# Differential attention: softmax weights combined in one pass on VectorE, weight splits held back on GpSimd, and the gate's SiLU computed through tanh

## The reference

```python
q, k, v, g_attn, x_lru, g_lru = split(rmsnorm(x) @ w_in)     # 8 heads; q, k: 2 x 64 per head; v: 128
for i in range(8):                                           # 128 queries against (i + 1) * 128 keys
    s = einsum(q_i, k[:end]) * 64 ** -0.5                    # two score maps c = 0, 1 per head
    p = softmax(where(causal, s, -inf))
    w = p[:, :, 0] - lam * p[:, :, 1]
    out_i = w @ v[:end]
o = rmsnorm(out, subln_g) * (1 - lam_init)
y_attn = o * silu(g_attn)
```

## Time and profile before

| what | value |
|---|---|
| timed runs | 3614.07, 3614.57 (median), 3616.83 us |
| profiled execution, first to last instruction (span) | 3615.4 us |
| PE busy | 3342.6 us (92%) |
| DVE busy | 1509.8 us (42%) |
| ACT busy | 867.8 us (24%) |
| POOL busy | 952.1 us (26%) |
| mean granted TensorE clock | 0.958 |

### The profile page before, as it was taken

One profiled execution on the slowest core, in us unless ns is written; L12 is line 12 of the kernel. 1 busy time (PEld: TensorE's weight loads), 2 busy tenths in 40 slices (PEclk: granted clock), 3 DMA queues, 4 the chain that ended last, 5 costly groups with the idle time before them and its releaser, 6 DMA issues.

```text
span 3615.4 us, 40852 instructions
## 1 busy us (share of the span) xinstructions
PE 3342.6 (92%) x15618; PEld 2741.2 (76%) x15618; DVE 1509.8 (42%) x1960; ACT 867.8 (24%) x1359; POOL 952.1 (26%) x514
## 2 busy tenths in 40 slices
PE   6999889887797998989999999889999989999999
PEld 5777777776585777768788888768787768888887
DVE  6775555556535566630121223222612542323232
ACT  4454334343202323221122222211201020101010
POOL 2331111111131221113222222134233323333332
PEclk9999999998998999889999999999999989999999
DMA  3220000000244111101211221231112101111112
GB/s 124 96 70 30 30 25 30 25 30 12 83 136 149 36 52 70 53 24 46 98 47 56 71 62 55 68 106 59 46 47 85 55 30 49 50 46 46 52 46 75
DMA packets 83705, 214.19 MB, mean 59 GB/s; under 512 B 7024, under 2 KB 33264, under 8 KB 83456
## 3 DMA queue, kind: packets, MB, share of 16 engines
q1 hardware_dynamic: 48176, 167.27, 14.1%
q10 hardware_dynamic: 35408, 45.24, 4.0%
HBM read 193.44 MB, written 19.04 MB: 59 GB/s over the span
## 4 chain that ended last, share of the span: by engine, by line
PE 79%; DVE 12%; ACT 4%; issue 3%; DMA 1%; ACTq 0%; PEld 0%; POOL 0%; DVEq 0%; PEldq 0%; POOLq 0%
PE proj_bank L208 20%; PE proj_bank L210 20%; PE proj_bank L209 20%; PE aux_banks L208 2%; PE aux_banks L209 2%; PE aux_banks L210 2%; PE aux_banks L755 2%; PE aux_banks L762 1%; ACT att_p L870 1%; PE aux_banks L1815 1%; DVE att_p L970 1%; DVE aux_banks L959 1%; PE aux_banks L1498 1%; DVE att_p L969 1%; PE aux_banks L1839 1%
## 5 line engine op out<-in xcount | busy, mean ns | idle before, releaser
L208 PE MATMUL proj_bank<-h_hi,slab_hi 128*128 128x512 f32 x2816 | 1129.8, 401 | 35.9 <-DVE h_lo L381 9.1
L210 PE MATMUL proj_bank<-h_hi,slab_lo 128*128 128x512 f32 x2816 | 1110.5, 394 | 0.0
L209 PE MATMUL proj_bank<-h_lo,slab_hi 128*128 128x512 f32 x2816 | 1110.4, 394 | 0.0
L226 POOL CAST slab_hi<-slab_raw 128x1024 fp32r<-128x1024 f32 x255 | 275.9, 1082 | 2620.8 <-PE proj_bank L210 2270.9
L228 POOL TENSOR_TENSOR slab_lo<-slab_raw,slab_hi 128x1024 fp32r<-128x1024 f32 x255 | 676.3, 2652 | 20.4
L208 PEld LDWEIGHTS proj_bank<-h_hi,slab_hi 128*128 128x128 f32 x2816 | 538.9, 191 | 161.3 <-issue 25.3
L210 PEld LDWEIGHTS proj_bank<-h_hi,slab_lo 128*128 128x128 f32 x2816 | 537.0, 191 | 115.7
L209 PEld LDWEIGHTS proj_bank<-h_lo,slab_hi 128*128 128x128 f32 x2816 | 539.0, 191 | 110.0 <-issue 2.2
L208 PE MATMUL proj_bank<-ffn_hi,slab_hi 128*128 128x512 f32 x512 | 199.2, 389 | 0.0
L209 PE MATMUL proj_bank<-ffn_lo,slab_hi 128*128 128x512 f32 x512 | 199.2, 389 | 0.0
L210 PE MATMUL proj_bank<-ffn_hi,slab_lo 128*128 128x512 f32 x512 | 199.2, 389 | 0.0
(11 more groups left out here) (340 smaller groups left out, 4191.3 us busy)
## 6 DMA issues: line engine op xcount, KB each, us to landing
slab_raw<-wts SPq DMA_DIRECT2D x255, 512.0 KB, 3.4
ada_w<-ada_w SPq DMA_DIRECT2D x40, 384.0 KB, 3.6
ada_w_early<-ada_w SPq DMA_DIRECT2D x24, 384.0 KB, 3.5
ssd_decay_rows<-decay_sums ACTq DMA_DIRECT2D x16, 512.0 KB, 4.2
dil_rows<-dilated_out ACTq DMA_DIRECT2D x12, 520.0 KB, 7.9
x_first<-xT SPq DMA_DIRECT2D x4, 1024.0 KB, 9.2
x_again<-xT ACTq DMA_DIRECT2D x4, 1024.0 KB, 9.3
x_kept<-x ACTq DMA_DIRECT2D x8, 512.0 KB, 4.0
```

Source lines behind the costliest of these rows:

```text
L208: pe.matmul(bank, k.whi[:, slot, wk, :], hi[:, xk, cols], start=first and a == 0, stop=False)
L209: pe.matmul(bank, k.whi[:, slot, wk, :], lo[:, xk, cols], start=False, stop=False)
L210: mm = pe.matmul(bank, k.wlo[:, slot, wk, :], hi[:, xk, cols], start=False, stop=last and a == len(ks) - 1)
L226: pool.tensor_copy(k.whi[:, slot], k.raw[:, slot]).then_inc(k.s_hi, 1)
```

## The change

It has five parts.

1. The weights of a step are no longer normalised. With t0 and t1 the sums of the exponentials e0 and e1, VectorE makes e1 * (lam * t0 / t1) - e0 in one pass, which is -t0 times the old weights. The norm over the head's output removes the factor: its epsilon is multiplied by t0 squared, and the minus sign goes into the norm's gain `subg`.
2. Map 1 goes ahead of map 0 in scores, maxima and exponentials (`ORDER`), each map with its own reduce, masked maximum, `nmax` (128x1) and wait.
3. GpSimd's split of an attention slab also waits for the weights of a step (`weighed`): gate 0, v 1, q 3, k 5 steps into the head before. The slabs come in the order gate, v, q, k, so that q's is split before k's; the slots swap from head to head (`to`, `par`).
4. The gate: ScalarE computes tanh(g/2) into y, VectorE then (tanh + 1) * g with g still in the bank (`gate`, in steps 0 and 1 after `weights`), and the factor 0.5 goes into `subg`. The bank is free for the next half when VectorE is done (`att_gated`). Head 0 keeps SiLU and one ACT copy doubles it.
5. Semaphores are cleared and used again (28 clears on VectorE ahead of the second block).

```diff
-                pool.wait_ge(k.s_proj, slab * 2 - (2 - halves))
+                pool.wait_ge(k.s_proj, slab * 2 - 2 if done is None else done)
+            if weighed is not None:
+                pool.wait_ge(k.s_att_w, weighed)
...
+            freed, weighed = (-1, 0, 2, 4), (0, 1, 3, 5)
+            for s in range(4):
+                early = isinstance(h, int) and (h == 0 or h == 1 and s == 0)
+                one(h * 4 + (ATT_0 + s), s % 2, h * 2 + (ATT_0 + s) // 2, True, done=h * 8 + (2 * ATT_0 + freed[s]), to=(s + par) % 2,
+                    weighed=None if early else h * TT + (weighed[s] - TT))
...
-        dve.tensor_scalar(k.subg, param(k, "subln_g"), 1.0 - LAM_INIT, None, ALU.mult)
+        dve.tensor_scalar(k.subg, param(k, "subln_g"), 0.5 * (LAM_INIT - 1.0), None, ALU.mult)
...
-    SLAB = (0, 0, 1, 1, 3, 2, 2, 3)
+    SLAB = (0, 0, 1, 1, 2, 3, 3, 2)
+    ORDER = (1, 0)
...
+            elif i < 4:
+                pe.wait_ge(s_gated, h * 2 + (i - 1))
...
-            for c in range(2):
+            for c in ORDER:
...
-                act.activation(k.y[:, ds(h, 1), cols]..., bank, ACT.Silu).then_inc(s_evac, 1)
+                act.activation(k.y[:, ds(h, 1), cols]..., bank, ACT.Tanh, scale=0.5).then_inc(s_tanh, 1)
...
-            act.wait_ge(s_nmax, step + 1)
-            for c in range(2):
+            for n, c in enumerate(ORDER):
+                act.wait_ge(s_nmax, step * 2 + (n + 1))
...
+        act.activation(k.y[:, 0, :], k.y[:, 0, :], ACT.Copy, scale=2.0)
...
+            for n, c in enumerate(ORDER):
+                dve.wait_ge(s_score, step * 2 + (n + 1))
+                if early:
+                    v.settle(dve, dve.tensor_reduce(mx[:, c:c + 1], flat[:, c, 0:early], AX, ALU.max))
                 dve.sem_inc(s_seen, 1)
                 own = flat[:, c, early:keys]
+                v.settle(dve, dve.tensor_tensor_reduce(own, own, k.mask[...], 1.0, mx[:, c:c + 1] if early else LOWEST,
+                                                       ALU.add, ALU.max, mx[:, 2 + c:3 + c]))
+                dve.tensor_scalar(nmax[:, c:c + 1], mx[:, 2 + c:3 + c], -SCALE, None, ALU.mult).then_inc(s_nmax, 1)
...
+            dve.wait_ge(s_exp, step * 2 + 3)
+            v.settle(dve, dve.reciprocal(ratio, total[par][:, 1, i:i + 1]))
+            v.settle(dve, dve.tensor_scalar(ratio, ratio, k.lam, None, ALU.mult))
             dve.wait_ge(s_exp, step * 2 + 4)
+            v.settle(dve, dve.tensor_scalar(ratio, ratio, total[par][:, 0, i:i + 1], None, ALU.mult))
+            dve.scalar_tensor_tensor(p[:, 0, 0:keys], p[:, 1, 0:keys], ratio, p[:, 0, 0:keys], ALU.mult, ALU.subtract).then_inc(s_w, 1)
...
+            own = total[par][:, 0, :]
+            v.settle(dve, dve.scalar_tensor_tensor(epst, own, EPS, own, ALU.mult, ALU.mult))
             turned(turns)
-            dve.tensor_scalar(k.stat, turn[:, 0:TT], 1.0 / P, EPS, ALU.mult, ALU.add).then_inc(s_turn_free, 1)
+            dve.scalar_tensor_tensor(k.stat, turn[:, 0:TT], 1.0 / P, epst, ALU.mult, ALU.add).then_inc(s_turn_free, 1)
...
+        def gate(h, i):
+            cols = slice(CHUNK[i] * HALF, (CHUNK[i] + 1) * HALF)
+            yt = k.y[:, ds(h, 1), cols].rearrange("p a b -> p (a b)")
+            dve.wait_ge(s_tanh, h * 2 + (i - 1))
+            dve.scalar_tensor_tensor(yt, yt, 1.0, k.bank[i % 2][:], ALU.add, ALU.mult).then_inc(s_gated, 1)
...
+                if more and i < 2:
+                    gate(h + 1, i)
...
-        slabs += [slab(w1, 0, part * D + h * P) for part in (3, 2, 1, 0)]
+        slabs += [slab(w1, 0, part * D + h * P) for part in (3, 2, 0, 1)]
```

More of the change, by code:

```diff
@@ L131, in make_core, with again @@
     k.at, k.sem = at, sem
+    k.spent, k.cleared = [], []
+    def again(name):
+        return k.cleared.pop(0)
+    k.again = again
     k.raw = at("slab_raw", 0, [P, 2, KT, P])
@@ L234, in _ @@
                 one(i * 2 + s, s, i, True)
-        with pool.Fori(0, HEADS) as h:
-            for s in range(4):
-                one(h * 4 + (ATT_0 + s), s % 2, h * 2 + (ATT_0 + s) // 2, True, halves=1 if s == 0 else 0)
+        for h in range(2):
+            head(h, h)
+        with pool.Fori(1, HEADS // 2) as m:
+            for b in range(2):
+                head(m * 2 + b, b)
         for s in range(2):
-            one(OUT1_0 + s, s, OUT1_0 // 2, True, halves=1 - s)
+            one(OUT1_0 + s, s, OUT1_0 // 2, True, done=2 * OUT1_0 + s - 1, weighed=(HEADS - 1) * TT + s)
         with pool.Fori(OUT1_0 // 2 + 1, N_SLABS // 2) as i:
@@ L672, in attention_stage @@
     p = k.at("att_p", k.W + 36, [P, 2, T])
+    total = [k.small[:, a:a + 2 * TT].rearrange("p (c i) -> p c i", c=2) for a in (72, 100)]
+    epst = k.small[:, 116:116 + TT]
     wt = k.at("att_w_turned", k.W + 44, [P, TT, P])
[L674 removed]
+    nmax, ratio = k.small[:, 48:50], k.small[:, 52:53]
     mx = k.small[:, 64:68]
     score, turn, out = k.aux[:, 0:4, :], k.aux[:, 4, :], k.aux[:, 5, :]
[L677 removed]
+    s_evac, s_tanh, s_gated = k.sem("att_evacuated"), k.sem("att_tanh"), k.s_att_gated
     s_hi, s_low, s_both = k.sem("att_qk_high"), k.sem("att_qk_low"), k.sem("att_q_both_rows")
@@ L788, in recurrent @@
             for c in range(2):
-                project(k, pe, OUT1_0 + 1, 1, c, k.bank[c][:], k.yhi, k.ylo, [(t, t + KT)], first=t == 0, last=False, counts=False)
+                project(k, pe, OUT1_0, 0, c, k.bank[c][:], k.yhi, k.ylo, [(t, t + KT)], first=t == 0, last=False, counts=False)
         def one(h, par, after, more):
@@ L823, in _ @@
         for i in range(8):
-            half(0, i)
+            half(0, i, 0)
             if i in VALUES:
@@ L1056, in _ @@
         last.start = uses(HEADS) - 2
-        statistics(last, HEADS - 1)
+        statistics(last, HEADS - 1, (HEADS - 1) % 2)
         inverse(HEADS - 1)
@@ L1216, in _ @@
         dve.wait_ge(s_gain, 2)
+        for s in k.spent:
+            dve.sem_clear(s)
+    k.cleared, k.spent = k.spent, []
 def ssd_norm_stage(k, block):
@@ L2475, in pack @@
     for h in range(HEADS):
-        slabs += [slab(w1, 0, part * D + h * P) for part in (3, 2, 1, 0)]
+        slabs += [slab(w1, 0, part * D + h * P) for part in (3, 2, 0, 1)]
     for f in range(KT):
-        slabs += [slab(i["w_out"][0], half * D, f * P) for half in range(2)]
+        slabs += [slab(i["w_out"][0], half * D, f * P) for half in ((1, 0) if f == 0 else (0, 1))]
     slabs += [slab(w2, 0, at_dt, SSD_HEADS)]
```

73 lines of the change are left out of this document (33 added, 40 removed).

## The result

| | before | after |
|---|---|---|
| timed runs, median (lowest to highest) | 3615.70 (3614.07 to 3621.33), 4 runs | 3550.36 (3547.90 to 3550.91), 4 runs |
| ratio, with its 95% interval | | 0.9816 [0.9802, 0.983] |
| profiled execution, span | 3615.4 | 3546.1 |
| mean granted clock | 0.958 | 0.963 |

The kernel is 65 us faster by the medians and 69.3 us by the profiled spans. The forecast was 3541 with a range of 3527 to 3571, so the time lies inside, 9 us over the point and just above the 3535 to 3550 to which the prediction gave half of its chances. Of the 9 us, 5 are in the span (3546.1 for 3541.3), 1.8 are that an execution's time stands that much above its span (3547.9 for 3546.1), and 2.5 that the profiled execution was the fastest of the four.

What follows compares the result with a forecast made beforehand. TensorE held 79% of the chain, so time is won only where it stands still or runs at low clock. Gains of 24.0 + 2.6 + 15.0 - 5.1 + 23.7 + 4.9 + 9 = 74.1 us gave 3541 us, range 3527 to 3571.

Steps and rivals of the forecast that it cites:

- Step 7: TensorE's 3.53 us wait at step 7 of heads 0 to 6 goes but for 0.1 each: 24.0 us gained.
- Step 6: The 0.44 us wait at step 6 of heads 1 to 6 goes entirely: 2.6 us gained.
- Step 3: The 2.75 us wait ahead of step 3's turning in heads 1 to 6 shrinks to 0.25: 15.0 us gained.
- The new wait: In step 1 of heads 1 to 6, the gate on VectorE delays the statistics' copy by 0.85 us: 5.1 us lost.
- The clock: Low clock stretches vanish: 22 of 22.9 us in the looped heads plus 1.7 at head 7's start, 23.7 us gained.
- the clock stays low in part: Rival: the small waits left in steps 1 to 3 keep half the low stretches; gain 62 us, 3553 us; chance 0.20.
- One-column `nmax`: VectorE's `nmax`, now one column, is not stretched beside a split: 0 us; otherwise up to 2 us over the heads.
- Ahead of head 0: TensorE's 3.33 us wait for q's split and 1.6 us of low clock behind it go: 4.9 us gained.
- Head 7: The chain of VectorE and ScalarE that sets head 7's steps gets shorter: 9 us gained, bounds 4 and 15.5.
- My chains are too short: Rival: VectorE's order binds in steps 0, 2, 6, 7, head 7 gives only 5 us; gain 48, 3567 us; chance 0.21.
- Tanh shares Exp's table: Tanh needs no table load apart from Exp's; the rival that it does gives 3564 us, chance 0.05.
- The slower case: Rival: VectorE stands in step 1's gate behind ScalarE's queue, 14 us per head, 3620 us; slower or nothing had chance 0.04.

Runs made afterwards that it cites:

- no_hold: The kernel after, with GpSimd's splits no longer held back for the weights: 3551.04 us, ratio 0.9815.
- joint_max: The kernel after, with the maxima of both maps joint again ahead of a single two-column `nmax`, map 1 still first: 3555.28 us, ratio 0.9832.
- weights_only: The kernel after with SiLU on ScalarE, joint maxima, no hold-back and old slab order; combined weights, map 1 first, wait order and clears kept: 3560.87 us, ratio 0.9828.
- joint_no_hold: The kernel after, with joint maxima of both maps and also without GpSimd's hold-back: 3563.22 us, ratio 0.9848.
- silu_back: The kernel after, with the gate's SiLU back on ScalarE straight from the bank, no tanh and no gate on VectorE: 3540.40 us, ratio 0.9787.
- load_waits: The kernel after, with ScalarE's two waits ahead of the first exponential exchanged: 3549.14 us, ratio 0.9811.
- gate_later: The kernel after, with the gate's first VectorE operation moved behind step 1's copy and maxima: 3536.60 us, ratio 0.9779.
- old_order: The kernel after, with the slabs in the old order gate, v, k, q and fixed slots: 3551.13 us, ratio 0.981.
- hold_alone: The kernel before, with only the hold-back of GpSimd's splits for the weights added: 3599.51 us, ratio 0.9949.

## Why the prediction was right, and where it was off

- **Step 7, forecast 24.0.** The 3.53 us went, seven times. New are waits of 0.39 for the copy at step 7's second group: by the sums for heads 1 to 6, "DVE att_w_turned" went from 0.8 to 2.3 us, 1.5 off the gain. The size was right, its working was not. I gave 1.96 us per head to the hold-back; `no_hold` shows that without it nothing is lost. There the stretch is gone because the pass is ready earlier: one pass less, one maximum less ahead of it, a reciprocal that hides. It then starts before the split, with 0.40 to 0.56 us to spare. The same 1.96 us can be had from either side (`no_hold` and `joint_max` both have the pass at 1.28), and my sum credited one side alone. Without both (`weights_only`, `joint_no_hold`) the pass takes 2.12 or 2.13 and step 7 waits 0.78, so the single pass with map 1 first removes 2.75 of the 3.53 by itself. I had also put the pass over map 1 at 1.2, though its row has 1.52 beside GpSimd: 1.52, 1.96 and the 0.05 between the two passes already add up to 3.53.
- **Step 6, 2.6:** gone in full; the wait for `att_p` has no entry in the looped heads.
- **Step 3, 15.0.** I left 0.25 of the 2.75. In heads 1 to 6 the wait for the spreading went from 21.6 to 6.4 us, 15.2 less; with step 3's second wait of 0.84 as it was, (6.4 - 6 x 0.84) / 6 = 0.23 is left. That it comes so near to my 0.25 is luck. I took it for the rest of VectorE's chain, but that chain is no longer what ends last: y's spreading (607.09, and all twelve in these heads) waits for TensorE's own spreading matmuls (L808), 0.77 us after VectorE is free, while in the kernel before it followed the weights at once. The chain became shorter than I summed, and the 0.23 is TensorE's own round trip over VectorE. Of the terms, SiLU's load and Exp's earlier load were not both needed: with SiLU back (`silu_back`) and with Exp's load behind the maximum (`load_waits`) the wait for the spreading over the whole stage grew by 1.8 and 0.8 us only (11.7 to 13.5 and 12.5), of which 0.9 and 0.4 in heads 1 to 6 (6.4 to 7.3 and 6.8). One detail was wrong: Exp's load does not wait for `nmax` any more. The change also exchanged ScalarE's two waits, so that the load is issued ahead of the one for `nmax` (601.73).
- **The new wait, -5.1.** 0.80 us in each of six heads, 4.8 in all, forecast 0.85. The chain is as written: tanh at 0.60, the gate 0.69, the copy behind it.
- **The clock, 23.7. This is the step that failed.** The prediction said of the new wait that "It is like the 0.84, after which the clock did not fall", and took 22 of the 22.9 us of the looped heads. The windows of after still lack 0.02 x (73.1 + 74.9 + 75.1) + 0.05 x 74.5 = 8.2 us, so 14.7 came. In four of the six heads a low stretch begins 1.4 to 2.8 us after the end of the 0.80 us wait, with the one-column matmuls of the statistics in between. Taking away that wait (`gate_later`, `silu_back`) takes away all of them. What failed is thus the comparison: a wait of 0.84 us ahead of full matmuls was no measure for one of 0.80 ahead of one-column matmuls. This is the rival "the clock stays low in part", which had a chance of 0.20, though at a third and not at half of its price.
- **One-column `nmax`:** 0 was right; two columns would have been 1.6 us beside the split (`joint_max`).
- **Ahead of head 0, 4.9 (8.3 with its step 7).** 10.9 us. Of it 3.53 and 3.33 are the two waits; two small ones that the sum left out went too, 0.35 for a split and 0.36 at step 6. The clock from 257 us on went from 0.96 to 0.98, another 2.1 us (before it was low for 7.7 us up to the cut, after for 3.4), and 0.56 stood already at the first matmul of the projections (262.79 before, 262.23 after). The last 0.7 I have not assigned. The low stretch before (280.1 to 283.5) need not come with the wait for q's split: in `old_order` and `weights_only` that wait is back, at 3.33 and 3.32 us, and none follows.
- **Head 7, 10.7 with the clock.** 9.0 us; the clock did not improve there (0.85 in both, over the whole stretch from step 7's turning to the output projection). The waits that the prediction bounded the gain by, 15.5 us, are 1.5 + 5.3 = 6.8 now, so 8.7 of them went; what is left is the chain of VectorE, as before.
- **The clears:** hidden, as forecast. With them ahead of it, VectorE's first operation behind TensorE's sums still found 6.71 us of idle time, for 6.61 in the kernel before.
- **The rivals.** "My chains are too short" did not happen: `joint_max` and `load_waits` lengthen them by a maximum and by a wait, and lose 5 us, within noise, and 0. Tanh shares Exp's table. The slower case had the right place (VectorE behind ScalarE in step 1) and the wrong size: 0.8 us and the clock, not 14.
- **The total.** The span is 4.8 us over the sum. The looped heads missed 5.3 and head 7 1.7, and 2.6 came ahead of head 0 from things that my sum left out or put too low: that part of the nearness is luck.

How the parts share the 65 us, by the runs: `weights_only` has 61 of them, with clock 1.00 in its looped heads. From there to `joint_no_hold`, 3563.2, come the order of slabs (4.2 us less in the trace) and the tanh (about 10 more), which by the medians are 2 us together; from that to the kernel after, 3550.4, the hold-back and the maxima map by map, 13 us less together, with intervals apart. Either of these two alone gives most of it by the medians: 3555.3 with the hold-back, 3551.0 with the separate maxima.

## What to carry to other kernels

A wait that a contended operation causes can be removed by making the other engine wait or by having the operation ready earlier; if a change does both, only one is worth its price, and a run that undoes each shows which. An operation put on an engine in front of something that TensorE needs costs its own length and what TensorE's clock does afterwards: place it behind what is awaited, here behind the next copy and maxima, for 14 us. Before counting a removed table load as gain, look whether the chain that it stands in still has the last word once the other parts are in.

## What the runs showed of the hardware that was not expected

**The race between VectorE and GpSimd goes by who starts first.** The 1024-key pass of two SBUF inputs takes 1.28 us when it starts first, even by 0.40 us, and the CAST then takes 1.78 for 1.04 (`no_hold`; 1.62 where the pass was 0.56 ahead). Started together with the CAST, within 0.01 us, it takes 2.13 to the CAST's 1.04 (12 of 12 such starts in `weights_only` and `joint_no_hold`); started within the TENSOR_TENSOR, 3.24. Each time the loser ends about its own length after the winner: 354.14 + 1.28 + 1.04 = 356.46 against the CAST's end at 356.32. The Trainium skill, page "SBUF — State Buffer", section "SBUF: two separate sides", states this as an exclusive lock: whichever operation starts first has the shared pair for the whole instruction and the other blocks. The traces agree, to within 0.2 us. The prediction had asked only whether there is a split beside the pass.

**The clock fell after a 0.8 us wait only next to one-column matmuls.** The stretch with the wait and most of the 16 one-column matmuls in head 1 of the kernel after, and the low ones of its heads 1 and 6:

```profile
371.00:374.60 3.60, 2.79 (x23) 2.46 (x22) 2.56 (x9) 1.44 (x4) 0.00 (x0) 1.00 0.00 0
374.60:378.00 3.40, 3.40 (x9) 2.66 (x10) 1.38 (x5) 0.33 (x2) 0.00 (x0) 0.50 0.00 0
739.80:746.60 6.80, 6.80 (x19) 5.52 (x19) 1.60 (x7) 0.67 (x2) 0.00 (x0) 0.50 0.00 0
```

Before the fall TensorE idled 0.81 us and ran the statistics at 2.4 GHz; then it ran full matmuls at 1.2 GHz. The rest is read from heads 1 to 6 of all kernels. Six of them have the wait of 0.80 or 0.81 us ahead of the statistics (the kernel after, `no_hold`, `joint_max`, `joint_no_hold`, `load_waits`, `old_order`), and a low stretch begins within 3 us of the end of that wait in 21 of 36 heads: 4, 3, 3, 4, 3 and 4. The other seven kernels have the same statistics without a wait, and none follows in 42 heads. Nor does one follow a wait of that size without the statistics: not the 18 in `weights_only`, nor the 0.80 to 1.16 at step 7 in `hold_alone`. Why it is 21 of 36 stays open. The only other low stretch there, outside the kernel before and `hold_alone` with their waits of 2.75 and more, is the one in `old_order` after 1.86 us of idle time. That the wait and the narrow matmuls must come together is read from these kernels, not from one that moves the statistics away from the wait; that was not tried.

**Of two waits ahead of an exponential, its table load stands behind the first only.** In the kernel after the wait for the turned weights comes first and that for `nmax` last, and the load runs before `nmax` is there (601.73, with 0.25 us of waiting behind it). With the two waits exchanged (`load_waits`) the load itself waited 1.61 us for `nmax`, as it had in the kernel before. The order of two waits thus places 1.28 us on or off the chain; here the chain had room for either.
